# One transformer block on one core: GpSimd's low-part subtraction of a weight unit, issued as two halves of 512 columns

## The reference

```python
x = x + 0.5 * swiglu(rmsnorm(x, ffn1_norm), ffn1_w_gu, ffn1_w_down)
x = x + token_mixing(rmsnorm(x, mix_norm), w_in, lower_bounds, hg_norm, conv_w, conv_norm, w_out)
x = x + cross_attention(rmsnorm(x, xa_norm), rmsnorm(mem, mem_norm), xa_wq, xa_wkv, xa_wo)
x = x + 0.5 * swiglu(rmsnorm(x, ffn2_norm), ffn2_w_gu, ffn2_w_down)
return rmsnorm(x, final_norm)

def swiglu(h, w_gu, w_down):
    gate, up = jnp.split(h @ w_gu, 2, axis=-1)
    return (jax.nn.silu(gate) * up) @ w_down
```

## Time and profile before

| | |
|---|---|
| Median of 3 runs | 1185.71 us (1184.31 to 1186.06) |
| Profiled execution: span, first to last instruction | 1183.3 us |
| Profiled execution: its own time beside the span | the page gives the span alone |
| TensorE busy | 1144.0 us, 97% |
| VectorE busy | 534.2 us, 45% |
| GpSimd busy | 494.9 us, 42% |
| ScalarE busy | 428.6 us, 36% |
| DMA, share of 16 engines | 27.9% on the main queue |
| Granted TensorE clock, mean | 0.991 |

### The profile page before, as it was taken

The page is one execution under the profiler, slowest core; times in us unless marked ns, Lnnn a source line. Parts: engine busy times, 40 slices in busy tenths (PEclk is TensorE's granted clock), DMA queues, the critical chain, the costliest instruction groups (busy, mean ns, idle before and its releaser), DMA issues.

```text
span 1183.3 us, 14737 instructions
## 1 busy us (share of the span) xinstructions
PE 1144.0 (97%) x5366; PEld 950.1 (80%) x5366; DVE 534.2 (45%) x660; ACT 428.6 (36%) x576; POOL 494.9 (42%) x208
## 2 busy tenths in 40 slices
PE   6999999999999999999998999998999999999997
PEld 4888888888887888787877888786888888888886
DVE  7433343442222567888478224456344334332222
ACT  6322332232222645554246543335232223222221
POOL 4444444444444333232325773134444444444440
PEclk9999999999999999999999999998999999999999
DMA  6323223223333222121222542122322322233312
GB/s 225 107 89 106 89 92 103 100 95 107 106 105 104 76 72 72 55 70 54 84 94 82 185 159 72 39 71 89 106 90 89 106 90 98 96 107 104 104 60 71
DMA packets 33317, 113.10 MB, mean 96 GB/s; under 512 B 3712, under 2 KB 5888, under 8 KB 33152
## 3 DMA queue, kind: packets, MB, share of 16 engines
q1 hardware_dynamic: 33136, 111.53, 27.9%
q10 hardware_dynamic: 144, 1.05, 0.3%
HBM read 110.47 MB, written 2.10 MB: 95 GB/s over the span
## 4 chain that ended last, share of the span: by engine, by line
PE 42%; issue 38%; POOL 16%; DVE 2%; ACT 1%; POOLq 0%; DVEq 0%; ACTq 0%
POOL wl L340 16%; PE bank L964 13%; PE bank L966 13%; PE bank L965 13%; DVE acc L642 1%; ACT xh L384 0%; DVE x L662 0%; PE score L964 0%; DVE x L956 0%; PE score L966 0%; PE score L965 0%; PE n_bank L1007 0%; POOLq L339 0%; PE o_bank L964 0%; ACT wh L352 0%
## 5 line engine op out<-in xcount | busy, mean ns | idle before, releaser
L340 POOL TENSOR_TENSOR wl<-raw,wh 128x1024 fp32r<-128x1024 f32 x204 | 494.7, 2427 | 662.0 <-ACT wh L352 349.2
L964 PE MATMUL bank<-xh,wh 128*128 128x512 f32 x952 | 378.0, 397 | 4.6 <-DVE xl L634 4.6
L966 PE MATMUL bank<-xh,wl 128*128 128x512 f32 x952 | 372.4, 391 | 0.0
L965 PE MATMUL bank<-xl,wh 128*128 128x512 f32 x952 | 372.4, 391 | 0.0
L365 ACT ACTIVATE wh<-raw 128x1024 fp32r<-128x1024 f32 x104 | 110.4, 1062 | 396.1 <-DVE ubuf L678 219.4
L964 PEld LDWEIGHTS bank<-xh,wh 128*128 128x128 f32 x952 | 179.9, 189 | 44.9 <-DVE xl L634 5.9
L965 PEld LDWEIGHTS bank<-xl,wh 128*128 128x128 f32 x952 | 180.0, 189 | 38.8 <-issue 2.0
L966 PEld LDWEIGHTS bank<-xh,wl 128*128 128x128 f32 x952 | 179.8, 189 | 38.0
L352 ACT ACTIVATE wh<-raw 128x1024 fp32r<-128x1024 f32 x99 | 104.3, 1053 | 140.0 <-PE bank L966 139.0
L964 PE MATMUL bank<-hid_h,wh 128*128 128x512 f32 (+1 forms) x374 | 141.0, 377 | 0.0
L966 PE MATMUL bank<-hid_h,wl 128*128 128x512 f32 (+1 forms) x374 | 140.8, 377 | 0.0
(11 more groups left out here) (209 smaller groups left out, 1081.7 us busy)
## 6 DMA issues: line engine op xcount, KB each, us to landing
raw<-w_all SPq DMA_DIRECT2D x204, 512.0 KB, 3.3
x<-x_t SPq DMA_DIRECT2D x8, 256.0 KB, 5.7
out_t<-x SPq DMA_DIRECT2D x8, 256.0 KB, 2.3
memf<-mem_t ACTq DMA_DIRECT2D x1, 1024.0 KB, 4.9
gbuf<-masks_d SPq DMA_DIRECT2D x1, 256.0 KB, 8.4
ident<-ident_d SPq DMA_DIRECT2D x1, 64.0 KB, 8.1
par<-params SPq DMA_DIRECT2D x1, 36.5 KB, 3.1
```

What stands on the lines that cost most here:

```text
L340: nc.gpsimd.tensor_tensor(wl[:, c, :], raw[:, c, :], wh[:, c, :].bitcast(f32), SUB)\
L964: nc.tensor.matmul(out_, a[0], b_[0], start=first, stop=False)
L965: nc.tensor.matmul(out_, a[0], b_[1], start=False, stop=False)
L966: return nc.tensor.matmul(out_, a[1], b_[0], start=False, stop=last)
```

## The change

GpSimd's instruction for a unit, 1024 columns wide, becomes two, of columns 0 to 511 and 512 to 1023. The wait for `hi_ready` stands before the first, `lo_ready` is counted up after the second. Nothing else is touched: neither semaphores and their counts nor any other engine's list.

```diff
             with pool.Fori(0, NU // SLOTS) as i:
                 for c in range(SLOTS):
                     pool.wait_ge(hi_ready, i * SLOTS + (c + 1))
-                    nc.gpsimd.tensor_tensor(wl[:, c, :], raw[:, c, :], wh[:, c, :].bitcast(f32), SUB)\
-                        .then_inc(lo_ready, 1)
+                    for half in (slice(0, UNIT // 2), slice(UNIT // 2, UNIT)):
+                        ins = nc.gpsimd.tensor_tensor(wl[:, c, half], raw[:, c, half], wh[:, c, half].bitcast(f32), SUB)
+                    ins.then_inc(lo_ready, 1)
```

## The result

The changed kernel takes 1171.53 us (1170.22 to 1172.4, 4 runs) against 1185.87 us, a ratio of 0.9877 with a 95% interval of 0.9858 to 0.9896: 14.6 us less (12.3 to 16.8). I had forecast 1176.7, 9.0 less, in a range of 1174.0 to 1186.3. The profiled execution has a span of 1168.4 us, 14.9 less than before.

A forecast was written before the change was run, and what follows sets the result against it. TensorE was taken to bound the kernel, its waits mostly for VectorE held behind GpSimd instructions. Terms 6.0 + 1.0 + 0.7 + 1.0 + 0.3 = 9.0 us gave 1176.7, range 1174.0 to 1186.3.

The forecast's parts named there:

- the turns: GpSimd and VectorE alternate on a shared port, one instruction each; halves shorten GpSimd's turn to 1.23 us.
- the sign of no turn: In the profile after, L642 keeping instances of 2.4 to 2.9 us would show VectorE not getting in between halves.
- The rival of no turn between the halves: Second half follows too closely for VectorE to get in; 1186.0 us (1185.7 to 1186.7), chance 0.20.
- The slower case: No turn between halves and 0.30 us extra on each of sixteen units: 4.8 us more, 1190.5; chance 0.08.
- the small gain: VectorE gets in, but behind `xa_wo` only the last L642's turn counts: 1.2 without clock, 1183.0 us; chance 0.10.
- The price of one more instruction: On GpSimd, splitting a unit costs 0.10 us extra, between nothing and 0.30; free where nobody waits.
- The loop behind `xa_wo`: At 779 to 815 us, TensorE's 3.95 us wait shrinks to 0.5 and the clock stays up: 6.0 (1.2 to 7.4).
- the 7.0 of the working: Behind `xa_wo`, 4.3 us from the wait and 2.7 from the clock, before lowering the term to 6.0.
- The recurrence: Held L785 makes TensorE wait 0.43 us at 512.19, again at 552; 0.5 gained each, 1.0 (0 to 1.2).
- the start of the mixing phase: There a TensorE wait of 0.35 us for `xl` goes: 0.3 gained (0 to 0.35).
- The loop behind `w_out`: Waits of 2.15 us at 622.38 and 2.56 at 641.99 shorten; 1.0 for both (-0.6 to +3).
- The start: TensorE's 3.94 us wait for the input's sum of squares shortens by 0.7 (0 to 1.0); the clock still falls.

The follow-up runs named there:

- halves in the four places alone: Against the kernel before, halves only for units 0 to 7, 68 to 107 and 132 to 139, all others whole: 1171.99 us.
- the run on two units: Against the kernel before, halves only for units 94 and 95, made just ahead of TensorE's wait for the transposed keys in the recurrence: 1182.91 us.

## Why the prediction was wrong

**What bounds the kernel, and the turns.** Right. VectorE instructions with two SBUF inputs stand behind a whole GpSimd instruction, and VectorE gets in between two of them even when the second waits for nothing. With halves L635 goes in before a second half that then takes 1.73 us, and halves in the four places alone carry all of the gain. With GpSimd's work cut to 16 columns `xl` and L642 are down to their shortest times behind the start, and 27.5 us go. L642's mean fell from 1369 to 1208 ns, not to the 1000 that I named as a sign: before 15 of the 43 were held, for 2.4 to 2.9 us in all, and now 24 take 1.4 to 1.8. But none takes more than that, where I had named 2.4 to 2.9 as the sign of no turn. The rival of no turn between the halves, to which I gave 0.20 and which the Trainium skill's sentence in "GPSIMD Engine Reference", section "Instruction dispatch" speaks for, did not come: the cores may each go on by themselves, but VectorE got its turn all the same. The slower case and the small gain did not come either.

**The price of one more instruction.** I took 0.10 us a unit between 0 and 0.30. (One reading in it was wrong: `xl` let go at 781.29 + 2.38 = 783.67, not 783.57, so the unit was held for 2.26 us and not 2.36. That takes 0.2 us off four turns.) The changed kernel's two halves stand alone in 2.54 us at 43.72, against 2.36 to 2.40 before, so 0.16; quarters take 2.82, three extra for 0.44. The estimate from the Trainium skill, "GPSIMD Engine Reference", section "Elementwise — side-by-side cycle accounting", 0.30, is nearly twice what was measured; the measurement decides. I wrote that the price is free where nobody waits, and four places in the changed kernel's trace do wait: TensorE loses 1.7 us there in all, of which my sum had a part behind `w_out` alone.

```profile
43.72 2.54 POOL L341 TENSOR_TENSOR wl<-raw,wh 128x512 fp32r<-128x512 f32 x2 [2.31 <-ACT wh L366]
```

```profile
52.44 2.82 POOL L344 TENSOR_TENSOR wl<-raw,wh 128x256 fp32r<-128x256 f32 x4 [0.52 <-ACT wh L373]
```

(The second row is of the kernel with quarters everywhere.)

**The loop behind `xa_wo`.** 6.6 (5.0 to 8.2) against my 6.0. The wait went and the clock with it, as forecast; the walk to it was wrong and the bound made it right. I had one turn saved on each of four long L642, 4.7 us less the price. In the changed kernel the last update comes 26.34 us behind the first (771.48 to 797.82), before 32.87 (779.52 to 812.39): 6.5 us sooner, by the other order shown above. TensorE could use only 4.7 of it, since then its own arrival binds, the upper bound that I had given (4.75). That this lies near my 4.3 is luck. The clock gave 2.5 against my 2.7. So the trace has 7.3 between 805 and 1052 us, and 0.5 of cost at 776 ahead of it; from the 7.0 of the working I had taken 1.0 off without a row behind it.

**The recurrence: the term that failed.** I put 1.0, two waits of 0.43, and 0.3 at the start of the mixing phase; it was 4.3 (2.7 to 5.8). The step that failed is the list of waits: places that end behind a held VectorE instruction were put at nothing. The largest is the wait of 2.7 us for `kdT` at 562, third among TensorE's waits for VectorE behind the two of 3.9 that I used, and followed by a slow clock. The prediction names 562 only among the places where GpSimd might cost time, with no term in the sum and no reason; the one that I wrote down ahead of the run on two units is that TensorE wants unit 95 next, and that was wrong. The two units split alone gave 3.4 us (2.3 to 4.5), of which the trace shows 1.1 as the wait and 1.5 as the clock. Then each of the two places at 512 and 552 had a second wait behind it, of 0.20 us for `kd` (L790), that went with the first. The distance grows by 1.1 us at each, where I took 0.5; that is more than the two waits shown, since TensorE's matmuls also overlap again (they follow each 0.23 us and are shown as 0.39 long). And the wait at 486, which falls from 1.5 to 0.9 us, I had not looked behind at all. In the trace of the kernel with halves in the recurrence alone these make 0.6 + 1.1 + 1.1 + 1.1 = 3.9 us with no change in the clock at 562, and 0.3 of cost is taken off. The start of the mixing phase gave 0.1 and not 0.3: the wait of 0.35 went and one of 0.26 for the sum came.

**The loop behind `w_out`.** I put 1.0 between -0.6 and 3; it was 2.4 (1.4 to 3.4). The traces have less than the runs: 1.2 us between 595 and 655 us, in the changed kernel, in the one with halves in this place alone and in the one with all four places. The wait at 622 fell by 1.3 us, where I took 0.8, that at 642 by 0.8, and TensorE lost 0.9 for units that came later. The clock gave nothing there. In the changed kernel it is as low behind the wait of 1.79 as it was before behind 2.56, only 8.5 us earlier on the time axis:

```profile
632.00:642.00 10.00, 8.46 (x58) 8.46 (x59) 7.91 (x9) 6.33 (x9) 8.45 (x7) 0.83 0.33 109
```

In the kernel with halves in this place alone it was 1.00 from 640 to 650, but then TensorE waited 0.46, 0.47 and 0.45 us for the next three units and was no better off at 655. What the other 1.2 us of the runs are stays open. (The profiled execution of that kernel was its slowest, 1184.98 against a median of 1183.61.)

**The start.** 0.7, and 0.9 (-0.4 to 2.1) measured. The kernel with halves in the four places, in which x came as late as before, has its first sum 0.7 earlier, and as much was still there at 380. I wrote that the clock still falls. It does in that kernel, behind a wait of 2.4 us (0.79 from 26 to 34 us), but it was 1.00 in the changed one behind 1.9 and in the one with halves at the start alone behind 3.3. So the clock there is not something that the halves can be shown to change.

**The range.** Its low end, 1174.0, added little to the likeliest case, since each term was bounded by its own walk and the place left out had no term. The sum of my upper bounds (7.4, 3, 1.0, 1.2, 0.35) was 13.0, which is 1172.8; I cut it at 11.7. The measured time lies under both. What no bound covered was the wait at 562 with its clock.

## What to carry to other kernels

Where a GpSimd instruction on SBUF lies beside VectorE's two-input instructions and TensorE waits for VectorE, divide GpSimd's instruction: in this kernel each division gave VectorE a turn for about 0.15 us of GpSimd's time, until GpSimd's own results came late, past four pieces of 256 columns. To size it, go through every wait of TensorE that ends on VectorE and walk back to a held instruction; and count from the code which unit a ring's consumer is at, before saying that the producer beside it is late. What the clock loses behind a wait goes into the range, not into the likeliest case, where the wait is of a length that has gone both ways: here 1.1 us off a wait came with 1.5 us of clock in one kernel and with none in another. And when two traces are compared by stretches, shift the stretch by the distance of the instructions first.

## What was not expected of the hardware

The same wait of TensorE did not always cost the same clock. Behind 1.34 us at 403 the granted clock was 1.00 before, behind 1.33 us it was 0.57 in the changed kernel, on the same instructions. Behind 1.6 us at 562 it was 1.00 in the changed kernel and in the one with two units, and low in the one with halves in the recurrence (0.72 from 558 to 564) and in the one with all four places; behind 2.16 us, with pieces of 768 and 256, it was 1.00. Behind the first sum it was 1.00 after 3.3 us in one kernel and 0.79 after 1.9 us in another (the one with 16 columns). Behind the 2.15 us at 622 it was 1.00 before, and 0.79 in the kernel with halves at the start alone, behind 2.2 us. The row of that kernel:

```profile
618.00:626.00 8.00, 5.83 (x19) 4.39 (x18) 6.65 (x11) 5.94 (x10) 3.37 (x2) 0.79 0.10 25
```

So the length of the wait ahead is not all that decides, and I took it for that when I let the clock of 622 vouch for others. What else does stays open; I did not try it. One such stretch costs 1.5 to 1.7 us of TensorE's time in these traces, so it may explain some of the scatter of 2 us between runs of one kernel, but that is argued, not shown.
